# Index scores and choice of keys moved beside the rotary tiles; attention over mixed token tiles; VectorE scales the outputs

## What is computed

```python
q = apply_rope(rmsnorm(q, q_gain), cos, sin)      # 16 heads of 64
k = apply_rope(rmsnorm(k, k_gain), cos, sin)
qi = apply_rope(qi, cos, sin)                     # 8 index heads of 64
ki = apply_rope(rmsnorm(ki, None)[:, :, None, :], cos, sin)[:, :, 0, :]
wi = wi.astype(f32) * (IDX_HEADS ** -0.5)
def attend_block(args):                           # blocks of 128 queries
    s_idx = jnp.einsum('bqhd,bkd->bqhk', qib, ki).astype(f32) * idx_scale
    score = jnp.einsum('bqhk,bqh->bqk', jax.nn.relu(s_idx), wb)
    score = jnp.where(causal, score, -jnp.inf)
    _, sel = lax.top_k(score, topk)               # 128 keys per query
    logits = jnp.einsum('bqhd,bqkhd->bhqk', qb, kg).astype(f32) * att_scale
    p = jax.nn.softmax(logits, axis=-1).astype(vg.dtype)
    return jnp.einsum('bhqk,bqkhd->bqhd', p, vg)
return out @ w_o
```

## Time and profile before

| | |
|---|---|
| three runs | 3184.81, 3186.45, 3213.09 us |
| median | 3186.45 us |
| the profiled execution's own time | 3193.29 us |
| its span | 3191.5 us, mean granted TensorE clock 0.938 |
| TensorE busy | 2930.1 us, 92% |
| VectorE busy | 1876.4 us, 59% |
| ScalarE busy | 1406.8 us, 44% |
| GpSimd busy | 217.7 us, 7% |

### The profile page before, as it was taken

One profiled execution on the slowest core, in us unless ns is written; L12 is line 12 of the kernel. 1 busy time (PEld: TensorE's weight loads), 2 busy tenths in 40 slices (PEclk: granted clock), 3 DMA queues, 4 the chain that ended last, 5 costly groups with the idle time before them and its releaser, 6 DMA issues.

```text
span 3191.5 us, 35348 instructions
## 1 busy us (share of the span) xinstructions
PE 2930.1 (92%) x12584; PEld 2247.2 (70%) x12584; DVE 1876.4 (59%) x2157; ACT 1406.8 (44%) x1858; POOL 217.7 (7%) x167
## 2 busy tenths in 40 slices
PE   7999999985899999999984678999989999989998
PEld 2548878765677777777773466888867766768887
DVE  3436643564988888888887754333249567343322
ACT  2323323223677777777775233222133344332321
POOL 1100100003930000000001000000001100000000
PEclk8999989995999999999997889999999965999999
DMA  6921722313898989899992812222221200112221
GB/s 229 331 76 60 288 75 93 111 65 150 319 344 354 387 354 387 352 387 352 387 360 74 106 43 76 93 103 96 93 74 67 79 27 1 37 69 99 99 93 66
DMA packets 90799, 546.88 MB, mean 171 GB/s; under 512 B 9232, under 2 KB 18848, under 8 KB 32384
## 3 DMA queue, kind: packets, MB, share of 16 engines
q1 hardware_dynamic: 79584, 485.65, 41.0%
q0 software_dynamic: 10816, 59.58, 5.4%
q10 hardware_dynamic: 288, 0.15, 0.0%
HBM read 516.51 MB, written 41.42 MB: 175 GB/s over the span
## 4 chain that ended last, share of the span: by engine, by line
PE 71%; DVE 15%; issue 6%; DMA 4%; ACT 3%; POOL 1%; SPq 1%; DVEq 0%; ACTq 0%; PEldq 0%; POOLq 0%
PE bank L336 39%; PE bank L274 6%; PE bank L1124 4%; PE bank L1128 4%; PE bank L1127 4%; DVE expert_low L2196 4%; PE bank L1363 2%; DMA arena<-in_we_stream 2%; PE bank L1355 1%; ACT expert_high L1559 1%; DMA arena<-in_mod 1%; PE bank L1343 1%; PE bank L1108 1%; DVE arena L2298 1%; DVE expert_x_low L2281 1%
## 5 line engine op out<-in xcount | busy, mean ns | idle before, releaser
L2196 DVE TENSOR_TENSOR expert_low<-arena,expert_high 128x2048 fp32r<-128x2048 f32 x291 | 683.4, 2379 | 102.3 <-ACT expert_high L1559 84.1
L1559 ACT ACTIVATE expert_high<-arena 128x1024 fp32r<-128x1024 f32 x582 | 596.9, 1057 | 212.3 <-PE bank L1124 120.5
L336 PE MATMUL bank<-high_b,weight_parts 128*128 128x512 f32 x1872 | 592.9, 398 | 30.4 <-DVE low_b L2434 16.2
L703 DVE TENSOR_TENSOR weight_parts<-ring_pages,weight_parts 128x1024 fp32r<-128x1024 f32 x185 | 226.9, 1227 | 556.0 <-ACT weight_parts L695 555.4
L695 ACT ACTIVATE weight_parts<-ring_pages 128x1024 fp32r<-128x1024 f32 x185 | 196.0, 1060 | 590.4 <-PE bank L336 547.0
L336 PEld LDWEIGHTS bank<-high_b,weight_parts 128*128 128x128 f32 x1872 | 352.5, 190 | 121.9 <-issue 37.2
L336 PE MATMUL bank<-low_b,weight_parts 128*128 128x512 f32 x832 | 324.8, 390 | 0.0
L1124 PE MATMUL bank<-expert_high,expert_x_low 128*128 128x512 f32 x768 | 309.4, 403 | 13.5 <-DVE expert_low L2196 9.9
L1127 PE MATMUL bank<-expert_high,expert_x_high 128*128 128x512 f32 x768 | 300.9, 392 | 0.0
L1128 PE MATMUL bank<-expert_low,expert_x_high 128*128 128x512 f32 x768 | 300.5, 391 | 0.0
L336 PE MATMUL bank<-hidden_parts,weight_parts 128*128 128x512 f32 x1056 | 240.0, 389 | 4.3 <-DVE hidden_parts L2480 4.3
(11 more groups left out here) (457 smaller groups left out, 4113.6 us busy)
## 6 DMA issues: line engine op xcount, KB each, us to landing
arena<-in_we_stream SPq DMA_DIRECT2D x294, 1024.0 KB, 6.4
ring_pages<-in_wb_stream SPq DMA_DIRECT2D x93, 1024.0 KB, 4.8
ring_pages<-in_wa_stream SPq DMA_DIRECT2D x49, 1024.0 KB, 4.8
arena<-in_mod POOLq DMA_DIRECT2D x16, 1024.0 KB, 6.7
xbuf<-arena POOLq DMA_DIRECT2D x25, 512.0 KB, 15.9
arena<-xbuf SPq DMA_DIRECT2D x17, 512.0 KB, 7.3
ybuf<-arena SPq DMA_DIRECT2D x16, 512.0 KB, 2.6
arena<-kd SPq DMA_DIRECT2D x8, 512.0 KB, 22.1
```

The lines of the kernel that those rows point to most:

```text
L336: ins = pe.matmul(o, lhsT, rhs, start=start, stop=stop)
L703: nc.vector.tensor_tensor(low, src, high.bitcast(F32), ALU.subtract).then_inc(weights_split, 1)
L1559: nc.scalar.activation(ehigh[c % HIGH_E][:, at], ring_e[c % RING_E][:, at], ACT.Copy) \
L2196: nc.vector.tensor_tensor(elow[c % RING_E][:], ring_e[c % RING_E], ehigh[c % HIGH_E][:].bitcast(F32), ALU.subtract).then_inc(weights_split ...
```

## The change

Four things are done together.

1. The order of the rotary tiles becomes index queries, index key, q, k, and the stream of weights follows. The small weights of the index heads are made in steps 5 and 6.
2. The 24 index products with their relus and weighted sums move into steps 8 to 19 of the rotary stage, two in each: tile 1 in steps 8 to 11, tile 2 in 12 to 15, tile 3 in 16 to 19. Each tile has a bias buffer of its own, in which score and rounds work in place.
3. The 48 rounds of the choice: 8 in steps 13 to 20 (one each), 12 in step 21 and 16 in step 22, put three and four at a time behind each low part of the value weights, and the last 12 in attention, in odd steps up to 23. VectorE's call for the second half of step 22's weights at the end of step 21 is gone; it comes first in step 22.
4. Attention takes the pairs two at a time in the order of tiles 1, 2, 1, 2, ... for the first 32 pairs, then 0, 3, 0 four times and tile 3 for the last eight pairs. ScalarE's two output scalings per pair of heads become one VectorE multiplication of 128x128 with the two reciprocals, in every second step, and the 64 reciprocals of one column become 32 of two.

```diff
@@ -74,7 +74,7 @@
-            ("dq", "col", 0, 8), ("dk", "col", 0, 8), ("dqi", "col", 0, 4), ("dki", "col", 0, 1),
+            ("dqi", "col", 0, 4), ("dki", "col", 0, 1), ("dq", "col", 0, 8), ("dk", "col", 0, 8),
             ("dv", "row", 0, 2), ("wo", "col", 0, 8), ("gu1", "col", 0, 2 * FFT), ("down1", "col", 0, 8)]
...
@@ -135,41 +135,51 @@
-ROPED = [("dq", j, True, 0) for j in range(KT)] + [("dk", j, True, 1) for j in range(KT)]
-ROPED += [("dqi", j, False, None) for j in range(4)] + [("dki", 0, True, None)]
+ROPED = [("dqi", j, False, None) for j in range(4)] + [("dki", 0, True, None)]
+INDEX_FIRST = len(ROPED) + 3
+ROPED += [("dq", j, True, 0) for j in range(KT)] + [("dk", j, True, 1) for j in range(KT)]
 NR = len(ROPED)
+INDEXED = [(t, i) for t in range(1, NTX) for i in range(IH)]
+
+
+def indexed_at(s):
+
+    return INDEXED[2 * (s - INDEX_FIRST):2 * (s - INDEX_FIRST) + 2] if s >= INDEX_FIRST else []
+
+
...
-PAIRS = [(t, h) for t in range(NTX) for h in range(AH)]
+assert sum(len(indexed_at(s)) for s in range(NR)) == len(INDEXED)
+
+PAIRS = []
+for _order in ((1, 2) * (AH // 2), (0, 3, 0) * (AH // 4) + (3,) * (AH // 4)):
+    for _n, _t in enumerate(_order):
+        PAIRS += [(_t, 2 * _order[:_n].count(_t) + i) for i in range(2)]
 NPAIR = len(PAIRS)
...
+TILE_DONE = {PAIRS.index((t, AH - 1)) + MIX_LAG: t for t in range(NTX)}
...
@@ -639,25 +649,24 @@
-        bias = [page(32, T), page(43, T)]
-        score = page(32.5, T)
+        bias = [page(first, (t + 1) * P) for t, first in enumerate((32, 37.75, 32.125, 32.5))]
...
@@ -900,18 +909,19 @@
+            pool.wait_ge(S["b_bias0"], 1)
+            nc.gpsimd.affine_select(out=bias[0], in_=bias[0], compare_op=ALU.is_ge, fill=-MASKED, base=0,
+                                    pattern=[[-1, P]], channel_multiplier=1).then_inc(S["b_masked"], 1)
             for s in range(NR):
                 pool.wait_ge(bank_done, JB[f"rot{s}"] + 1)
                 v = roped_tile(s)
                 nc.gpsimd.tensor_tensor(v, v, cossin[:, 0, :], ALU.mult).then_inc(S["b_turned_cos"], 1)
...
+                for t in range(1, NTX):
+                    if s < NR and (t, IH - 1) in indexed_at(s):
+                        pool.wait_ge(S["b_score_ready"], t)
+                        diagonal = bias[t][:, t * P:(t + 1) * P]
+                        nc.gpsimd.affine_select(out=diagonal, in_=diagonal, compare_op=ALU.is_ge, fill=MASKED, base=0,
+                                                pattern=[[-1, P]], channel_multiplier=1).then_inc(S["b_masked"], 1)
...
@@ -1294,21 +1304,29 @@
...
+                    for n, (t, i) in enumerate(indexed_at(s)):
+                        if s == INDEX_FIRST and n == 0:
+                            pe.wait_ge(S["b_rotated"], INDEX_FIRST - 3)
+                        ps = opened(f"ix{t}{i}")
+                        r = 64 * (i % 2)
+                        pe.matmul(ps[:, 0:(t + 1) * P], qiT[r:r + 64, i // 2, t * P:(t + 1) * P],
+                                  kiT[r:r + 64, 0:(t + 1) * P], start=True, stop=True).then_inc(bank_done, 1)
+                    if s == 5:
+                        ps = opened("wip")
+                        pe.wait_ge(S["small_operands"], 3)
...
                     t, h = PAIRS[s]
+                    pe.wait_ge(S["b_rotated"], NR - KT + h // 2 + 1)
                     ps = opened(f"lg{s}")
...
-                    if t < NTX - 1:
-                        if s == 1:
-                            pe.wait_ge(S["b_rotated"], NR)
-                        for i in index_heads(h):
-                            ps = opened(f"ix{t + 1}{i}")
...
@@ -1759,6 +1767,17 @@
...
+                    for t, i in indexed_at(s):
+                        ps = result(act, f"ix{t}{i}")
+                        if n_relu >= 2:
+                            act.wait_ge(relu_used, n_relu - 1)
+                        n_relu += 1
+                        copied(act, nc.scalar.activation(rl[:, i % 2, 0:(t + 1) * P], ps[:, 0:(t + 1) * P],
+                                                         ACT.Relu), S["b_relu_ready"], n_relu, f"ix{t}{i}")
...
@@ -1788,35 +1806,12 @@
...
-                if VALUE_LAG <= s < NPAIR + VALUE_LAG and (s - VALUE_LAG) % 2 == 1:
-                    k = s - VALUE_LAG
-                    name = f"av{k - 1}"
-                    act.wait_ge(av_done, k // 2 + 1)
-                    act.wait_ge(S["b_sums_ready"], k + 1)
-                    for n in (k - 1, k):
-                        t, h = PAIRS[n]
-                        ins = nc.scalar.activation(mixed_rows[t % 2][:, h * HD:(h + 1) * HD],
-                                                   psum[JB[name] % 8][:, h % 2 * HD:(h % 2 + 1) * HD], ACT.Copy,
-                                                   scale=rsm[:, n % 8:n % 8 + 1])
-                        ins.then_inc(S["b_o_ready"], 1)
-                    act.wait_ge(S["b_o_ready"], k + 1)
-                    act.sem_inc(free(name), 1)
...
@@ -2495,14 +2490,45 @@
+            link(nc.vector.memset(bias[0], 0.0))
+            dve.sem_inc(S["b_bias0"], 1)
+
+            def index_score(t, i):
+
+                n = IH * (t - 1) + i + 1
+                w = (t + 1) * P
+                dve.wait_ge(S["b_relu_ready"], n)
+                if i == 0:
+                    ins = nc.vector.tensor_scalar(bias[t], rl[:, i % 2, 0:w], wi[:, t, i:i + 1], None, ALU.mult)
+                else:
+                    ins = nc.vector.scalar_tensor_tensor(out=bias[t], in0=rl[:, i % 2, 0:w], scalar=wi[:, t, i:i + 1],
+                                                         in1=bias[t], op0=ALU.mult, op1=ALU.add)
+                ins.then_inc(relu_used, 1)
+                dve.wait_ge(relu_used, n)
+                if i == IH - 1:
+                    dve.sem_inc(S["b_score_ready"], 1)
+
+            chosen = [0]
+
+            def choose(n):
+
+                for _ in range(n):
+                    t, at = 1 + chosen[0] // (TOPK // 8), chosen[0] % (TOPK // 8)
+                    if t == NTX:
+                        return
+                    chosen[0] += 1
+                    if at == 0:
+                        dve.wait_ge(S["b_masked"], t + 1)
+                    link(nc.vector.max(m8[:], bias[t]))
+                    link(nc.vector.match_replace(bias[t], m8[:], bias[t], TAKEN))
+                    if at == TOPK // 8 - 1:
+                        link(nc.vector.tensor_scalar(bias[t], bias[t], TAKEN / 2, -MASKED, ALU.is_gt, ALU.mult))
+
             for s in range(NR + 2):
...
                 if s >= NR:
-                    weights_low_part(dve, half_of("dv", s - NR, KT, True) + 1, split_to)
+                    for q in range(4):
+                        weights_low_part(dve, half_of("dv", s - NR, KT, True) - 2 + q, split_to)
+                        choose(3 + s - NR)
...
@@ -2516,8 +2542,6 @@
...
                     weights_low_part(dve, ahead("dv", ROPED[s][0], ROPED[s][1]), split_to)
-                elif s == NR:
-                    weights_low_part(dve, ahead("dv", "dv", 0, KT, True), split_to)
                 if s >= 2:
...
@@ -2527,49 +2551,42 @@
...
-            def scale_rows(s):
-
-                b = s % 4
-                dve.wait_ge(S["b_exped"], s + 1)
-                if s >= 8:
-                    dve.wait_ge(S["b_o_ready"], s - 7)
-                nc.vector.reciprocal(rsm[:, s % 8:s % 8 + 1], sm[:, b:b + 1]).then_inc(S["b_sums_ready"], 1)
+                if s == 6:
+                    ps = result(dve, "wi")
...
+                if s < NR:
+                    for t, i in indexed_at(s):
+                        index_score(t, i)
+                    if s >= INDEX_FIRST + 5:
+                        choose(1)
+            def outputs_scaled(k):
+
+                t, h = PAIRS[k - 1]
+                name = f"av{k - 1}"
+                dve.wait_ge(S["b_exped"], k + 1)
+                link(nc.vector.reciprocal(rsm[:], sm[:, (k - 1) % 8:k % 8 + 1]))
+                dve.wait_ge(av_done, k // 2 + 1)
+                copied(dve, nc.vector.tensor_tensor(
+                    mixed_rows[t][:, h * HD:(h + 2) * HD].rearrange("p (h d) -> p h d", h=2),
+                    psum[JB[name] % 8][:, 0:2 * HD].rearrange("p (h d) -> p h d", h=2),
+                    rsm[:].unsqueeze(2).to_broadcast([P, 2, HD]), ALU.mult), S["b_o_ready"], k // 2 + 1, name)
+
...
@@ -2579,26 +2596,17 @@
...
-                    nc.vector.tensor_tensor_reduce(pp[:, b, 0:w], ps[:, 0:w], bias[t % 2][:, 0:w], 1.0, 3.0e38,
+                    nc.vector.tensor_tensor_reduce(pp[:, b, 0:w], ps[:, 0:w], bias[t], 1.0, 3.0e38,
                                                    ALU.add, ALU.min, nmx[:, b:b + 1]).then_inc(S["b_logits"], 1)
                     dve.wait_ge(S["b_logits"], s + 1)
                     dve.sem_inc(free(name), 1)
-                if 1 <= s <= NPAIR:
-                    scale_rows(s - 1)
...
-                if s < NPAIR and t < NTX - 1:
-                    w = (t + 2) * P
```

(47 more changed lines are left out.)

105 lines of the change are left out of this document (29 added, 76 removed).

## The result

The changed kernel takes 3238.34 us (median of 4 runs, 3233.53 to 3242.3) against 3199.77 us for the kernel before (4 runs, 3184.81 to 3220.45). The ratio is 1.0128, with a 95% interval of 1.0073 to 1.0183: slower by 1.3%. The times of the kernel before fall into two groups (here and beside the experiments 3177 to 3193 us at a mean granted clock of 0.937 to 0.943, and 3213 to 3225 us at 0.927 to 0.930), so what follows is read from stages of the profiled executions: 3233.53 us after (span 3231.6) against 3193.29 before.

The account below looks back on a forecast made before the run. It took TensorE to bound the rotary stage and, at half clock, most of attention. Rotary +34, value stage +9 and attention -21 made +22 us on the median 3186.45: 3208.5 us, own range 3195 to 3225.

Parts of the forecast that it names:

- The rotary stage, +34: Rotary stage: VectorE's sums, rounds and a wait through ScalarE's relu and root start the value stage 34 us later.
- the bounds (+23 and +40): Rotary stage: +23 if nothing of the relu loop shows, +40 if the relus wait for TensorE too.
- The rival that the loop costs nothing: Rotary stage: the loop through the relu is hidden, growth 23 instead of 34 us, 3197.5 us in all; chance 0.12.
- The value stage, +9: Value stage: VectorE's remaining work, 58.6 us against 49.8, sets the end instead of TensorE; +9 us.
- The pause of TensorE, 7 us: Before attention: TensorE idles about 7 us behind VectorE's late work, so attention begins at 1.2 GHz.
- the clock stays up: Attention: after a short idle stretch TensorE keeps 2.4 GHz, first half 42 us less, 3166.5 us in all; chance 0.18.
- 2 + 97.6: Attention's first half: 2 us filling up, then 97.6 us for 32 pairs of tiles 1 and 2 at half clock.
- Attention, -21: Attention, first logits to `wo`: 166.5 us instead of 187.8, first half at half clock, second at full clock.
- The second 32 pairs at full clock ... make 54: Attention's second half: 16 steps of tile 3 at 2.48 us and 16 of tile 0 at 0.9, 54 us.
- The rival "the clock doesn't rise at the turned rows": Attention's second half stays at half clock, 94 us, 40 more than forecast, 3248.5 us in all; chance 0.22.

Follow-up runs that it names:

- the last run: Narrow-product kernel (512 columns in four steps) with eight rounds moved from the rotary loop to attention, tile order and added products adjusted; median 3164.84 us, ratio 0.9918 to the kernel before.

## Why the prediction was right or wrong

The forecast was 3208.5 us, and slower was in it with a third of the chances. The median lies 30 us above it; of that 13 us is the kernel before itself, 3199.77 in this comparison against 3186.45. That is outside the forecast's own range (3195 to 3225) and inside the wide one (3158 to 3248) only because that one takes in the rival with the clock that never rises; the sum itself had one of its terms wrong. By steps:

- **The rotary stage, +34: right, mechanism and size.** Steps of index tiles were to take 118.8 us in all and took 121.9, 9.2 to 10.8 us apart for the 9.6 to 10.2 named, between the bounds (+23 and +40). The chain last sum, relu, root, reciprocal stands in the timelines above, 1.66 us for the "about 1.5" of the forecast, and four buffers took it away. The rival that the loop costs nothing is ruled out. VectorE's wait for the root is 1.22 to 1.62 us in the steps without a round and 0.57 to 0.95 in those with one, since the round fills the rest.
- **The value stage, +9: right in its reading.** VectorE sets its end: moving four rounds gave 6.8 us. Rotary and value stage together were forecast at +43 and came to +47.7; 3 of the missing 5 us are in the rotary steps.
- **The pause of TensorE, 7 us: right in size** (7.49 us), **wrong in its part.** I took it for the reason that the clock is low in the first half, and gave the rival "the clock stays up" its chance on whether the pause would be short. With the pause at 1.97 us, and with it filled, the clock fell all the same. The first half at half clock came out as forecast (96.7 us to 2706.0 for 2 + 97.6), but for another reason: the kernel's steps don't hold 2.4 GHz even when they start in it.
- **Attention, -21: the step that failed.** "The second 32 pairs at full clock ... make 54", and with turned rows, 3 us until the rise and the run to `wo` 66.5 us. It took 91.4 us from 2706.0, so the -21 became +0.3. The clock did rise behind the turned rows, as in the earlier trace rows, but for 3.4 and 6.8 us, and then for the last 15.3. I had read tile 3's full clock in the kernel before as a property of its steps, and a rise as something that lasts. Tile 3 alone, at half clock for 66.1 us in the run with one tile after another, shows that it isn't. The kernel before itself had a counterexample that I passed over, in tile 2 (columns as in the earlier trace rows):

```profile
2659.00:2672.00 13.00, 11.15 (x66) 7.61 (x65) 9.73 (x25) 8.54 (x22) 0.29 (x1) 1.00 0.00 0
2672.00:2723.00 51.00, 51.00 (x157) 33.39 (x156) 30.52 (x85) 19.22 (x54) 0.00 (x0) 0.50 0.00 1
```

The clock was up for 13 us and then down for 51 in steps with no gap. At full clock the second half is near what I said: 74.8 us in the last run, with 256 and 64 columns more in each step.

- **The rival "the clock doesn't rise at the turned rows"** had the outcome nearly right (3248.5, and the profile after is 40.2 us above the one before, where it said 62 above the median) and the reason half: the clock rises and isn't kept. The Trainium skill ("TensorE: Matmul & The Clock Gate", "Part 4: PE-mode transpose") says that transposes don't count as busy like products. The traces don't settle it. In the changed kernel all three rises come right behind eight transposes in a row (clock 1.00 from 2710.4, 2717.2 and 2782.1), and the steps that didn't hold the clock are products for the greater part. But in the kernel before the turned rows begun at 2613.2 brought no rise, and the rise in tile 2, at 2659.3, came ahead of its turned rows (2662.1); with one tile after another the rows begun at 2703.5 and 2738.5 brought none. So turned rows are neither enough for a rise nor needed for one.

What the runs leave open: why thin steps bring the clock down. They have products on 64 of 128 rows, on 64 columns, and transposes, each behind a weight load of its own, and I didn't vary these one by one. Shown is that an added product in each step keeps it (128 columns beside tiles 1 and 2, 256 and 64 beside tiles 0 and 3, once the first four steps had 512), and that it fell 7.6 us behind the last added product where they stopped.

## What to carry to other kernels

A busy share of 100% says nothing about the clock: read the granted clock of each stretch beside it, and where small products run at 1.2 GHz by themselves, treat their work as twice as dear. Other engines' work beside them is mostly hidden, but not always: the output scaling moved back to ScalarE went with 9.2 us more. Taking work off an engine that isn't the limit there moves nothing; this change emptied VectorE in a stretch where TensorE's clock set the time, and paid for it in two stages where VectorE's time was the end of the path. Where a rise of the clock was seen once, ask for a second stretch with the same steps before counting on it.

## What the runs showed of the hardware that I had not expected

- TensorE's records fill 58.1 of 58.1 us and the granted clock is 0.50. Products that compute nothing, one a step, made the whole faster: the clock stayed at 0.99 to 1.00 and attention fell from 188.1 to 144.7 us with them in it. With products in the first eight steps alone, and the other edits the same, attention took 186.7 us and the span was 3208.0 us; with them in every step 148.4 and 3173.7.
- Filling a pause with dense products kept the clock up to its end, but not for long: 5.6 us of thin steps behind it, it was down.
- A float32 product of 384 columns took 0.75 us at 2.4 GHz, in two records. The rounds of the choice beside such products were hidden: TensorE was busy for 65.00 of 65.00 us and VectorE for 38.87.
